# Retention: values centered by ScalarE as they leave PSUM, a head norm without mean passes, the last pair's gate times norm weights made ahead, search bits moved

## The reference

```python
h = rms_norm(x, pre_mix_g)
r_q, r_k, r_v, r_g, a_q, a_c, i_q, i_k, i_w = split_cols(h @ w_in)   # 4 x 512, 512, 128, 512, 64, 8
# retention, 8 heads of 64 columns, chunks of 128 rows
rq, rk = rotate(r_q), rotate(r_k)
ry = retention_chunkwise(rq, rk, rv)      # (scores * decay) @ v + (q * xi) @ state, linear in v
# layer_norm over the 64 columns of a head, with gain and bias
mu = mean(ry, -1); var = mean(square(ry - mu), -1)
ry = (ry - mu) * rsqrt(var + EPS) * ret_norm_g + ret_norm_b
y_ret = silu(r_g) * ry
# sparse attention: an indexer scores all keys for each row, the best 256 are attended to
iscore = einsum(relu(einsum(qi, ki)), wi)  # causal, then top 256
...
x = x + rms_norm(concat([y_ret, y_dsa]) @ w_out, post_mix_g)
# then a SwiGLU FFN and a gated input embedding, untouched by the change
```

## Time and profile before

| | |
|---|---|
| median of three runs (lowest to highest) | 1431.73 us (1429.45 to 1433.17) |
| span of the profiled execution | 1428.3 us |
| own time of the profiled execution beside its span | none is given but the three runs |
| TensorE busy | 1376.4 us (96%) |
| VectorE | 1013.1 us (71%) |
| ScalarE | 605.1 us (42%) |
| GpSimd | 329.0 us (23%) |

### The profile page before, as it was taken

How to read it: one execution, slowest core, us unless ns; L and a number is a source line. 1 busy time by engine, 2 the same in 40 slices (tenths; PEclk the granted TensorE clock), 3 DMA queues, 4 the chain that set the end, 5 groups by cost and what they waited for, 6 DMA issues and landing times.

```text
span 1428.3 us, 19391 instructions
## 1 busy us (share of the span) xinstructions
PE 1376.4 (96%) x7142; PEld 1125.8 (79%) x7142; DVE 1013.1 (71%) x1592; ACT 605.1 (42%) x1229; POOL 329.0 (23%) x383
## 2 busy tenths in 40 slices
PE   7999999999989889998999999999999999999998
PEld 7887888887777567777778888888887888888886
DVE  5748789998999546765877777777776765565633
ACT  6434552315823776574522222222222656453221
POOL 4545457711541475652000000000000000000000
PEclk9999999999999999999999999999999999999999
DMA  6322223225323021133234555444458866662211
GB/s 215 82 56 71 79 84 116 94 92 192 111 101 143 31 74 61 45 91 107 55 131 165 177 177 177 161 148 153 156 193 289 316 239 223 237 213 75 67 53 45
DMA packets 137150, 189.02 MB, mean 132 GB/s; under 512 B 12768, under 2 KB 75616, under 8 KB 137056
## 3 DMA queue, kind: packets, MB, share of 16 engines
q1 hardware_dynamic: 120224, 152.17, 32.5%
q10 hardware_dynamic: 16832, 35.61, 6.5%
HBM read 130.08 MB, written 57.67 MB: 131 GB/s over the span
## 4 chain that ended last, share of the span: by engine, by line
PE 79%; DVE 7%; issue 4%; ACT 4%; POOL 3%; DMA 1%; DVEq 1%; SPq 0%; ACTq 0%; POOLq 0%
PE ps L728 23%; PE ps L729 23%; PE ps L730 23%; PE ps L930 2%; PE ps L922 2%; PE ps L941 1%; PE ps L769 1%; POOL mxs L2721 1%; DMA raw<-in_w_in 1%; DVE sc L1915 1%; ACT lm L1444 1%; DVEq L1931 1%; PE ps L857 1%; PE ps L892 1%; PE ps L855 1%
## 5 line engine op out<-in xcount | busy, mean ns | idle before, releaser
L2593 POOL TENSOR_TENSOR smf<-smf,sml 128x1 f32<-128x1 f32 x16 | 9.1, 579 | 739.3 <-DVE smf L2474 625.2
L728 PE MATMUL ps<-bh,ah 128*128 128x512 f32 x308 | 120.1, 390 | 2.4 <-DVE u2b L2315 2.4
L730 PE MATMUL ps<-bh,al 128*128 128x512 f32 x308 | 119.9, 389 | 0.0
L729 PE MATMUL ps<-bl,ah 128*128 128x512 f32 x308 | 119.8, 389 | 0.0
L728 PE MATMUL ps<-wbh,xth 128*128 128x512 f32 (+1 forms) x320 | 118.9, 371 | 0.0
L729 PE MATMUL ps<-wbl,xth 128*128 128x512 f32 (+1 forms) x320 | 117.7, 368 | 0.0
L730 PE MATMUL ps<-wbh,xtl 128*128 128x512 f32 (+1 forms) x320 | 117.7, 368 | 0.0
L2421 DVE TENSOR_TENSOR al<-ra,ah 128x512 fp32r<-128x512 f32 x77 | 53.1, 690 | 70.7 <-ACT ah L1671 70.3
L728 PE MATMUL ps<-th,ssh 128*128 128x512 f32 x240 | 93.6, 390 | 1.8 <-DVE u2b L2291 1.2
L730 PE MATMUL ps<-th,ssl 128*128 128x512 f32 x240 | 93.4, 389 | 0.0
L729 PE MATMUL ps<-tl,ssh 128*128 128x512 f32 x240 | 93.4, 389 | 0.0
(11 more groups left out here) (375 smaller groups left out, 3871.1 us busy)
## 6 DMA issues: line engine op xcount, KB each, us to landing
raw<-in_w_in SPq DMA_DIRECT2D x49, 256.0 KB, 3.0
wt<-in_w_ffn_down SPq DMA_DIRECT2D x44, 256.0 KB, 7.2
down_sums<-wt ACTq DMA_DIRECT2D x44, 256.0 KB, 5.0
ra<-hidden_sums SPq DMA_DIRECT2D x44, 256.0 KB, 2.9
rb<-down_sums SPq DMA_DIRECT2D x44, 256.0 KB, 3.5
raws<-in_w_ffn_gate SPq DMA_DIRECT2D x21, 512.0 KB, 3.9
raws<-in_w_ffn_up SPq DMA_DIRECT2D x21, 512.0 KB, 5.3
ret_rows<-stg SPq DMA_DIRECT2D x32, 320.0 KB, 3.4
```

The costliest lines, as they stand in the source:

```text
L728: pe.matmul(o, ah, wh, start=start, stop=False, skip_group_check=resumes)
L729: pe.matmul(o, ah, wl, start=False, stop=False, skip_group_check=resumes)
L730: return pe.matmul(o, al, wh, start=False, stop=stop, skip_group_check=resumes)
```

## The change

1. **The mean.** ScalarE now reads each head's 64 value columns of a retention unit twice. The first activation copies them, scaled by -1/64, and sums the result into a column of `vmean` (minus the mean). The second, behind a wait for those sums, adds that column as a bias (`Identity`) and writes the centered values. The one copy of both heads' values is gone.
2. **The norm.** `ret_center` becomes `ret_variance`, without the sum, its scaling and the subtraction.
3. **The last pair.** `last_ret_gains` makes silu times bias (into O[1]) and silu times gain (in place); `last_ret_gained` then multiplies and adds. Two passes ahead of the root and three behind it stand where four stood behind it. The variance of the last pair is made after the third Y, where it was made ahead of the third pair's four passes.
4. **The search bits.** Five steps stand between the pairs (one more behind the first Y, one more behind the second), seven in the mix stage.

The semaphore `a_sq` is renamed `a_acc`.

```diff
--- before.py
+++ after.py
@@ -109,7 +109,7 @@
     at = 0
     for name, n in (("ss0", 8), ("v0", 8), ("rs0", 8), ("half", 16), ("ssn", 16), ("vn", 16), ("rsn", 16),
                     ("mu", 8), ("pos", 8), ("sum", 16), ("rsum", 16), ("nmax", 4), ("ssm", 8), ("vm", 8),
-                    ("rsm", 8), ("ssf", 8), ("vf", 8), ("rsf", 8), ("vn_last", 16), ("rsn_last", 16)):
+                    ("rsm", 8), ("ssf", 8), ("vf", 8), ("rsf", 8), ("vn_last", 16), ("rsn_last", 16), ("vmean", 4)):
         cols[name] = SML[:, at:at + n]
         at += n
     assert at <= 256
@@ -270,7 +270,7 @@
         return PS[:, 512 * i:512 * i + n]
 
 
-    names = """a_sq v_var p_rs v_xn t_xt a_xh v_xl v_ang a_trig a_whi v_qlo a_kh v_kl p_wlo t_unit a_ev
+    names = """a_acc v_var p_rs v_xn t_xt a_xh v_xl v_ang a_trig a_whi v_qlo a_kh v_kl p_wlo t_unit a_ev
         v_link p_link v_nrm p_nrs t_nt a_nt t_ix a_rl v_acc p_caus v_mask p_tri p_rot
         t_rb a_rb t_sc a_st p_st t_ro a_o a_silu p_zero v_lnv p_lnr v_y t_yr a_yrt
         t_lg v_lm a_ex t_tp a_tp t_pv v_rs a_bs a_rs v_ms t_vt a_vt a_mss p_mr x1_made a_fss p_fr fn_made
@@ -324,7 +324,7 @@
 
     SEARCH_A, SEARCH_B = (B0 + 1, B0 + 2), (B0 + 3, B0 + 4, B0 + 5)
     SIGN = 31
-    BITS_AHEAD, BITS_BETWEEN, BITS_MIX = 20, 3, 9
+    BITS_AHEAD, BITS_BETWEEN, BITS_MIX = 20, 5, 7
     PIECES = 3 * len(SEARCH_B)
 
     PIECES_AT = {13: 1, 21: 1, 29: 1, 37: 2, 45: 2, 53: 2}
@@ -1261,8 +1261,8 @@
         def square(r):
             act.wait_ge(load_x[r], 16)
             if r:
-                act.wait_ge(s["a_sq"], r)
-            sc.activation(pair(3), XN[r][:, :], ACT.Square, accum_out=cols["ss0"][:, r:r + 1]).then_inc(s["a_sq"], 1)
+                act.wait_ge(s["a_acc"], r)
+            sc.activation(pair(3), XN[r][:, :], ACT.Square, accum_out=cols["ss0"][:, r:r + 1]).then_inc(s["a_acc"], 1)
 
         def x_hi(r):
             act.wait_ge(s["t_xt"], r + 1)
@@ -1279,6 +1279,9 @@
                 act.wait_ge(s["t_unit"], KT * (c - 1))
             w = width(c)
             sc.copy(WBH[c % 2][:, k, 0:w], RAW[raw_slot(n)][:, 0:w]).then_inc(s["a_whi"], 1)
+
+        def value_slot(n, h):
+            return STG[n % 2][:, RV + 192 * h:RV + 192 * h + HD]
 
         def evacuate(g):
             c, u = divmod(g, KT)
@@ -1299,13 +1302,18 @@
                     act.wait_ge(s["load_const"], 64)
                 if n >= 2:
                     act.wait_ge(st_ret[n % 2], 16 * (n // 2))
+                for h in range(2):
+                    sc.activation(value_slot(n, h), o[:, 2 * P + h * HD:2 * P + (h + 1) * HD], ACT.Copy, scale=-1.0 / HD,
+                                  accum_out=cols["vmean"][:, 2 * (n % 2) + h:2 * (n % 2) + h + 1]).then_inc(s["a_acc"], 1)
                 for j in range(4):
                     c0 = H * (j // 2) + 2 * hp + j % 2
                     col = SCL[:, n % RT, c0:c0 + 1]
                     sc.activation(STG[n % 2][:, j * HD:(j + 1) * HD], o[:, j * HD:(j + 1) * HD], ACT.Copy, scale=col)
-                v01 = STG[n % 2][:, RV:RV + 384].rearrange("p (h c) -> p h c", h=2)[:, :, 0:HD]
-                sc.copy(v01, o[:, 2 * P:3 * P].rearrange("p (h c) -> p h c", h=2))
                 ins = sc.copy(STG[n % 2][:, RG_:RG_ + P], o[:, 3 * P:4 * P])
+                act.wait_ge(s["a_acc"], RT + 2 * (n + 1))
+                for h in range(2):
+                    ins = sc.activation(value_slot(n, h), o[:, 2 * P + h * HD:2 * P + (h + 1) * HD], ACT.Identity,
+                                        bias=cols["vmean"][:, 2 * (n % 2) + h:2 * (n % 2) + h + 1])
             ins.then_inc(s["a_ev"], 1)
 
         square(0)
@@ -1850,7 +1858,7 @@
 
         for r in range(RT + 2):
             if r < RT:
-                dve.wait_ge(s["a_sq"], r + 1)
+                dve.wait_ge(s["a_acc"], r + 1)
                 v.tensor_scalar(cols["v0"][:, r:r + 1], cols["ss0"][:, r:r + 1], 1.0 / D, EPS, ALU.mult, ALU.add)\
                  .then_inc(s["v_var"], 1)
             if r >= 2:
@@ -2021,7 +2029,7 @@
             search_step(SEARCH_B, m, JUNKB)
 
 
-        def ret_center(hp):
+        def ret_variance(hp):
 
             o16 = O[hp % 3][:, :, :].rearrange("p r (h e) -> p (r h) e", h=2)
             t16 = PT1[:, :, :].rearrange("p r (h e) -> p (r h) e", h=2)
@@ -2030,9 +2038,6 @@
             if hp >= 1:
                 dve.wait_ge(s["v_lnv"], hp)
             dve.wait_ge(s["a_o"], RT * (hp + 1))
-            link(v.tensor_reduce(cols["ssn"], o16, AX.X, ALU.add))
-            link(v.tensor_scalar(cols["ssn"], cols["ssn"], 1.0 / HD, None, ALU.mult))
-            link(v.tensor_tensor(o16, o16, cols["ssn"].unsqueeze(2).to_broadcast([P, 2 * RT, HD]), ALU.subtract))
             link(v.tensor_tensor(t16, o16, o16, ALU.mult))
             link(v.tensor_reduce(cols["ssn"], t16, AX.X, ALU.add))
             v.tensor_scalar(cols[norm_cols(hp)[0]], cols["ssn"], 1.0 / HD, EPS, ALU.mult, ALU.add).then_inc(s["v_lnv"], 1)
@@ -2053,6 +2058,21 @@
                     dve.wait_ge(s["t_yr"], hp)
                 v.tensor_tensor(Y[:, :, :], o, SGR[hp % 2][:, :, :], ALU.mult).then_inc(s["v_y"], 1)
 
+        def last_ret_gains():
+
+            sg = SGR[(NP - 1) % 2][:, :, :]
+            gain, shift = (g[:, (NP - 1) * P:NP * P].unsqueeze(1).to_broadcast([P, RT, P]) for g in (RG, RB))
+            dve.wait_ge(s["a_silu"], NP)
+            link(v.tensor_tensor(O[1][:, :, :], sg, shift, ALU.mult))
+            link(v.tensor_tensor(sg, sg, gain, ALU.mult))
+
+        def last_ret_gained():
+
+            o = O[(NP - 1) % 3][:, :, :]
+            link(v.tensor_tensor(o, o, SGR[(NP - 1) % 2][:, :, :], ALU.mult))
+            dve.wait_ge(s["t_yr"], NP - 1)
+            v.tensor_tensor(Y[:, :, :], o, O[1][:, :, :], ALU.add).then_inc(s["v_y"], 1)
+
         def last_ret_lo():
             for half in range(2):
                 rs = slice(half * 512, (half + 1) * 512)
@@ -2065,18 +2085,21 @@
             v.tensor_tensor(WOL[:, k, :], WOR[:, k, :], WOH[:, k, :].bitcast(F32), ALU.subtract)\
              .then_inc(s["v_wol"], 1)
 
+        between = iter(range(SIGN - BITS_AHEAD, BITS_MIX - 1, -1))
         for hp in range(NP - 1):
-            ret_center(hp)
-            search_step(SEARCH_B, SIGN - BITS_AHEAD - hp, JUNKM)
+            ret_variance(hp)
+            search_step(SEARCH_B, next(between), JUNKM)
             if hp >= 1:
                 out_weights_lo(2 * hp - 2)
                 out_weights_lo(2 * hp - 1)
-            if hp == NP - 2:
-                ret_center(NP - 1)
             for step in range(4):
                 ret_scale(hp, step)
-        for step in range(4):
-            ret_scale(NP - 1, step)
+            if hp < NP - 2:
+                search_step(SEARCH_B, next(between), JUNKM)
+        last_ret_gains()
+        ret_variance(NP - 1)
+        ret_scale(NP - 1, 0)
+        last_ret_gained()
 
         def query_parts(b):
             dve.wait_ge(s["a_qhi"], b + 1)
```

## The result

The changed kernel took 1438.82 us in the median of four runs (1438.75 without the outlier named below), against 1432.13 us in the median of four runs of the kernel before. The ratio is 1.0050, with a 95% interval of 1.0036 to 1.0063: slower by 5 to 9 us. One of the four runs, of 3513 us, is left out of the ratio. The forecast was 1437.0 us (1431.0 to 1441.0), slower.

A forecast was written before the change was run, and what follows sets the result against it. It took TensorE to bound the kernel, other engines mattering only where it waits. Evacuation 0.85 plus fourth Y 4.46 gave +5.3 us on the 1428.3 us span; with 3.4 us carried over for timed runs, 1437.0 us (1431.0 to 1441.0).

The forecast's parts named there:

- The wait at the third Y and its half clock: TensorE's 2.25 us wait before the third Y's transposes goes, and most likely the half clock behind it, 1.70 us.
- The fourth Y: VectorE's last Y is done at 420.4 us, 3.6 us later than before; TensorE waits 6.7 us for it.
- two meetings: Two of VectorE's last three passes each run beside a GpSimd low part, 0.96 us lost each, 1.92 counted.
- The half clock: TensorE's clock halves for one 3.4 us stretch from the fourth Y's transposes on: 1.70 us (0 to 3.4).
- The evacuation: ScalarE's unit grows 0.97 us, delaying GpSimd's rotation and VectorE's pick rounds in the indexer stage: +0.85 us (0.6 to 1.2).
- Rival D: Sums serialise ScalarE to over 2 us per unit; the store loop falls behind from 212 us: +6, 1443 us; chance 0.07.
- Search bits: Two of nine steps leave the mix stage, 7.5 us of VectorE, worth 0 under TensorE's full stage.
- my reason for the bits between the pairs: Each added search step puts 3.77 us on VectorE's chain; second Y at 389.2 us, third Y at 406.6.
- The forecast sum: 0.85 us from the indexer stage plus 4.46 us at the fourth Y: +5.3 us.

The follow-up runs named there:

- e1: Kernel before with only the changed evacuation; norm functions, their order and search bits as before: 1432.21 us, ratio 1.0009.
- e5: Changed kernel with the last pair's variance ahead of the two gate passes: 1436.28 us, ratio 1.0037.
- e6: Changed kernel without the gate passes made ahead; the last pair is scaled in four passes behind the root: 1436.97 us, ratio 1.0040.
- e7: Changed kernel with GpSimd's two low parts of the third pair waiting for the fourth Y: 1436.35 us, ratio 1.0032.
- e3: Changed kernel with the last pair's variance back ahead of the third pair's four passes: 1430.17 us, ratio 0.9991.
- e8: Changed kernel with 64 transposes of the identity on TensorE ahead of its wait for the fourth Y: 1436.48 us, ratio 1.0035.
- e2: Changed kernel with the old evacuation, so nobody subtracts the mean: 1437.99 us, ratio 1.0051.
- e4: Changed kernel with the old search bits, 3 between the pairs and 9 in the mix stage: 1438.09 us, ratio 1.0048.
- v1: e3 with the old search bits, 3 between the pairs and 9 in the mix stage: 1429.61 us, ratio 0.9987.
- v3: v2_gains_early with the causal mask ahead of the rotation in GpSimd's program: 1426.93 us, ratio 0.9968.
- e9: e4 with GpSimd's roots of pairs 1 and 2 at chunk steps 19 and 29 instead of 21 and 31: 1432.21 us, ratio 1.0003.
- v2_gains_early: e3 with search bits 4 and 8, gate passes ahead of the last variance, GpSimd's last low part of pair 1 before pair 2's root: 1429.26 us, ratio 0.9983.

## Why the prediction was right, point by point

**The wait at the third Y and its half clock** went as forecast: -2.4 and -1.6 against -2.25 and -1.70. The second is in part luck: it is the 3.4 us stretch of one execution, and behind the same wait e1's execution ran at half clock for 6.8 us.

**The fourth Y** followed the forecast chain link by link: gate passes 2.5, variance 2.7, idle for the root 3.0 (3.1), three passes 5.7 (5.6) with two meetings. e5, e6 and e7 each removed one link and got its price in the trace, e3 several at once. It came at 423.25 instead of 420.4; 1.2 of that is the start of the program, 0.5 the evacuation (which the sum carried apart), and 1.1 a third meeting that the chain missed: the third pair's `o<-o,sml` pass met the low part behind the root of pair 2. Two of the three last passes met one low part each, as counted, and as the Trainium skill's exclusive lock would have it (SBUF — State Buffer, "SBUF: two separate sides"); e7 agrees with the lock too, since both sides get their time back when they don't meet (VectorE 2.0 us, GpSimd 0.96). GpSimd's root doesn't act by that rule: in e3 it takes 3.81 us while VectorE's passes beside it take 1.22 and 1.23, so it does not hold them for its whole length.

**The half clock** was the term that was mis-sized most: 2.8 us instead of 1.70. I took one stretch of today's 3.4 us, beginning with the transposes; it lasted 10.25 us, of which 4.35 lay in the wait and cost nothing, and 5.9 in work. In e8's trace, with the idle time filled, all of it is gone.

**The evacuation**: the mechanism (rotation, mask, pick rounds) was right, the size 0.55 instead of 0.85. The unit grew by 0.63 us, not 0.97: the sum of 64 columns takes 0.20 us, below the floor of 0.25 that I set from a copy of 128 columns and a read. e2 takes the 0.5 away. Rival D, the store loop, did not come: ScalarE waits for the store five times instead of three, and TensorE is busy 118.00 of 118 us in that stretch. (The prediction names one such wait before, at 273.41; there are two from 212 us on, the other of 3.91 us at 218.07.)

**Missed in the loop**: 0.7 us that I set to nothing. TensorE waits 0.98 us at 391.01 for GpSimd's select, where it waited 0.59 before, and 0.23 at 384.77. e2 has the same waits, e1 the old ones, so it comes from VectorE's new order; that it is the selects meeting VectorE's passes I only argue from their rows, and did not try: the select behind the root of pair 1 takes 1.09 us (383.62) beside a weight split, where it took 0.41 (381.85) just behind one.

**Search bits** out of the mix stage were worth 0, as forecast: `keys_lo` waits for ScalarE's `keys_hi` 11.1 us instead of 1.47, so VectorE only idles longer. e4 and v1 confirm it. But my reason for the bits between the pairs (3.77 us each on the path of the third Y) was wrong: with them gone the third Y comes at the same time (e4). The forecast sum was hardly hurt, as the steps filled idle time that I had not counted either. That is luck: VectorE's work and the root of pair 2, which I had left out, ended within 0.1 us of each other (403.22 and 403.28).

The median moved by 6.7 us against 5.3 forecast.

## What to carry to other kernels

What lies behind the last long wait of another engine has to stand ahead of it: put the producer of a slow helper's input (here the variance for the root) first, and the work that needs nothing from it behind. A lighter engine gains nothing while the helper's queue place decides: moving three instructions was worth 8.6 us, two search steps 0. Before a producer is slowed, count who stands in line behind it on every queue that it feeds; turning that line around gained more than the slower producer had cost.

## What the runs showed of the hardware

A wait need not be listed to cost time: TensorE's matmuls of 128x512 that another engine has just released take 0.50 us instead of 0.39; with what stands ahead of them TensorE falls back 0.1 to 0.25 us at each without an entry among the waits, and 0.4 where there is one. That they were released just then is argued; in v3, with the pick rounds earlier, one of them is left. After idle stretches of 2.25, 2.27, 2.30 and 7.07 us TensorE ran at half clock for 3.4 (before), 6.8 (e1), 5.7 (e9) and 5.9 us (changed kernel); after 0.56 and 1.10 us it did not (v2_gains_early). The same idle stretch does not always end alike: behind 1.32 us at 652.33 the kernel before ran at half clock until 655.55, and behind the same 1.32 us at 660.75 the changed kernel stayed at full clock. When GpSimd's two-input passes (1.27 us alone) and VectorE's (1.23 us) meet, each meeting adds about 1 us to VectorE's pass (2.17 to 2.28), and the same GpSimd root takes 3.81 us beside VectorE's passes and 2.90 us alone, with those passes at 1.22 and 1.23 us.
